# First rows turned at once, tile 0's norms moved ahead of other work, the last V sets halved between two engines

## What is computed

```python
n = rms_norm(h, attn_norm);  proj = n @ w_in          # c_q, c_kv, k_rope, dq, dk, dv
y_mla  = mla(...)      # 8 heads, q and k normed and rotated, causal softmax
y_diff = diff_attn(...)  # 4 heads, a = softmax1 - lam * softmax2; y normed (subln)
h = h + concat(y_mla, y_diff) @ w_out
x = rms_norm(h, ffn_norm)                             # "h1" in the kernel
q = x @ w_query;  s = q . sub_keys                    # PEER: 8 heads, 2 x 128 keys
best, flat = top16 of the 16 x 16 pair sums;  experts = e1 * 128 + e2
g = softmax(best);  act = gelu(x . u[experts])
h = h + sum over 8*16 slots of g * act * v[experts]   # gathers of 128 rows x 4 KB
```

## Time and profile before

| | us |
|---|---|
| three runs | 1487.81, 1499.03, 1493.09 (median 1493.09) |
| profiled execution, its own time | 1485.78 |
| its span, first to last instruction | 1484.1 |
| PE, DVE, POOL, ACT busy | 1214.9, 1040.1, 579.8, 425.3 |
| start to first gather issued | 206.3 |
| first gather to the last V set added (L2166 ends) | 206.3 to 894.2 |
| next block, to the end of the span | 894.2 to 1484.1 |

### The profile page before, as it was taken

How to read it: one execution, slowest core, us unless ns; L and a number is a source line. 1 busy time by engine, 2 the same in 40 slices (tenths; PEclk the granted TensorE clock), 3 DMA queues, 4 the chain that set the end, 5 groups by cost and what they waited for, 6 DMA issues and landing times.

```text
span 1484.1 us, 17603 instructions
## 1 busy us (share of the span) xinstructions
PE 1214.9 (82%) x6525; PEld 878.9 (59%) x6525; DVE 1040.1 (70%) x1910; ACT 425.3 (29%) x741; POOL 579.8 (39%) x644
## 2 busy tenths in 40 slices
PE   6987996687786555566765578999999999999997
PEld 3545674344443222222222237989889999899997
DVE  5786468888688775866656646677778888665556
ACT  1147213021112110211111114333345555343332
POOL 4140026777777777777777742001010000000000
PEclk9999898789998888777777789999999999999999
DMA  9917149999999999999999987778759565345662
GB/s 324 359 50 255 55 169 349 396 409 405 409 409 407 407 404 400 409 409 410 409 409 410 409 338 246 255 270 282 266 190 324 185 208 176 114 142 187 204 200 74
DMA packets 179996, 435.45 MB, mean 293 GB/s; under 512 B 13913, under 2 KB 84642, under 8 KB 179926
## 3 DMA queue, kind: packets, MB, share of 16 engines
q0 software_dynamic: 84384, 306.26, 52.5%
q1 hardware_dynamic: 94502, 126.18, 25.4%
q10 hardware_dynamic: 1040, 2.10, 0.4%
HBM read 433.44 MB, written 2.14 MB: 294 GB/s over the span
## 4 chain that ended last, share of the span: by engine, by line
PE 42%; POOL 30%; issue 11%; DVE 9%; DMA 5%; ACT 3%; SPq 0%; DVEq 0%; POOLq 0%
POOL arena L797 22%; PE quad L1507 13%; POOL ring L797 7%; PE quad_a L1613 7%; PE quad_a L1521 6%; DMA ring<-in_ffn_w_gu_dram 3%; PE quad_a L1307 2%; PE quad L1289 2%; PE quad_a L1206 2%; PE quad_a L1461 2%; PE quad_a L1678 2%; PE quad_a L1693 1%; DMA arena<-in_w_ada_dram 1%; PE quad_a L1535 1%; DMA arena<-in_peer_v_dram,arena 1%
## 5 line engine op out<-in xcount | busy, mean ns | idle before, releaser
L1461 PE MATMUL quad_a<-arena 128*128 128x512 f32 x384 | 205.9, 701 | 119.2 <-DMA arena<-in_peer_v_dram,arena 119.2
L1461 PEld LDWEIGHTS quad_a<-arena 128*128 128x128 f32 x384 | 85.8, 228 | 238.6 <-issue 238.3
L797 POOL DMA_INDIRECT arena<-in_peer_v_dram,arena x193 | 186.6, 967 | 60.7 <-issue 57.8
L1507 PE MATMUL quad<-u_hi,w_hi 128*128 128x256 f32 x704 | 198.8, 282 | 3.3 <-DVE u_lo L2044 3.3
L1507 PE MATMUL quad<-u_lo,w_hi 128*128 128x256 f32 x704 | 198.7, 282 | 0.0
L1507 PE MATMUL quad<-u_hi,w_lo 128*128 128x256 f32 x704 | 198.6, 282 | 0.0
L1983 DVE TENSOR_TENSOR w_lo<-ring,w_hi 128x2048 fp32r<-128x2048 f32 x66 | 150.8, 2290 | 62.3 <-ACT w_hi L995 62.0
L797 POOL DMA_INDIRECT arena<-in_peer_u_dram,arena x168 | 170.3, 1014 | 58.1 <-issue 50.6
L989 ACT ACTIVATE arena<-ident,arena 128x128 f32<-128x128 f32 x192 | 59.6, 389 | 341.9 <-DVE arena L2149 341.9
L2159 DVE SCALAR_TENSOR_TENSOR hx<-arena,hx 128x1024 f32<-128x1024 f32 x46 | 59.1, 1285 | 136.3 <-DMA arena<-in_peer_v_dram,arena 136.0
L2142 DVE CUSTOM_DVE_ANT_0 arena<-arena,quad_a 128x1024 f32<-128x1024 f32 x123 | 147.2, 1219 | 8.1 <-DMA arena<-in_peer_u_dram,arena 4.8
(11 more groups left out here) (387 smaller groups left out, 2394.0 us busy)
## 6 DMA issues: line engine op xcount, KB each, us to landing
ring<-in_ffn_w_gu_dram SPq DMA_DIRECT2D x44, 1024.0 KB, 8.9
arena<-in_w_ada_dram POOLq DMA_DIRECT2D x60, 512.0 KB, 6.6
ring<-in_ffn_w_down_dram SPq DMA_DIRECT2D x22, 1024.0 KB, 5.0
ring<-in_w_mix_in_dram SPq DMA_DIRECT2D x20, 1024.0 KB, 7.1
arena<-in_peer_w_query_dram SPq DMA_DIRECT2D x4, 2048.0 KB, 9.7
ring<-in_w_ada_dram POOLq DMA_DIRECT2D x12, 512.0 KB, 11.8
arena<-in_w_in_dram SPq DMA_DIRECT2D x3, 2048.0 KB, 35.8
arena<-in_w_out_dram SPq DMA_DIRECT2D x2, 2048.0 KB, 11.5
```

The lines of the kernel that those rows point to most:

```text
L797: gp.indirect_dma_start(out=rows_of(n), out_offset=None, in_=t["peer_" + kind][0], in_offset=bass.IndirectOffsetOnAxis(ap=expert[tt][:, sl ...
L1461: last = te.matmul(sum_side[tt][:, cols], diag[:, i % DIAGS], rows_of(n)[:, cols], start=(slot == pe_slots[0]), stop=(slot == pe_slots[-1] ...
L1507: last = te.matmul(psum[c][:, w * SEQ:(w + 1) * SEQ], weight[a][:, k, (c % 2) * P:(c % 2 + 1) * P], (u_hi, u_lo)[b][:, k], start=(k == 0 a ...
```

## The change

1. **Start.** x's tile 0 is squared, normed and turned before the others; the gains' turn moves from lane d to lane a and comes after it; six of the 16 small gain loads (`gain_src[3:]`) move from SP's queue to ACT's, behind the 2 MB load. PE does chunk "c" of tile 0 before it turns x's tiles 1 and 2.
2. **y of tile 0.** Its squares come before weighted(5), its root on ACT before turned_out(4), its norm and turn still in step 6; PE waits for it, turns it and does values(4) ahead of scores(7). turn_probs(5) moves behind write_out(0, 0), turn_probs(6) behind values(5), values(6) and values(7) behind the turn of hn.
3. **h1 of tile 0 by halves.** Squares of half 0 after the first half of the output, put into the root as its bias; hn is written in two instructions, each with a count of its own.
4. **Fewer DVE steps in `pick`**, and for two heads `row_of` is one reduction instead of four adds.
5. **The last 16 slots of tile 1** go in turn to PE and DVE (8 and 8) instead of 12 and 4.

```diff
@@ -127,6 +127,7 @@
 small = sb("small", 256)[:]
+h1_half, h1_bias = small[:, 200:201], small[:, 201:202]
@@ -251,10 +252,12 @@
+    if (tt, slot) >= (QT - 1, SLOTS - 2 * GB):
+        return slot % 2 == 0
     return slot % 4 != 3
-pe_slots = [slot for slot in range(SLOTS) if on_pe(0, slot)]
-diag_at = {(tt, slot): i for i, (tt, slot) in enumerate((tt, slot) for tt in range(QT) for slot in pe_slots)}
+pe_slots = [[slot for slot in range(SLOTS) if on_pe(tt, slot)] for tt in range(QT)]
+diag_at = {(tt, slot): i for i, (tt, slot) in enumerate((tt, slot) for tt in range(QT) for slot in pe_slots[tt])}
 diag_list = list(diag_at)
@@ -431,16 +434,16 @@
-d_jobs = ["gains"] + [("nT", tt, b) for tt in range(3) for b in range(2)] + [("fill", 0), ("fill", 1)] + [("cT", tt) for tt in range(3)]
+d_jobs = [("nT", tt, b) for tt in range(3) for b in range(2)] + [("fill", 0), ("fill", 1)] + [("cT", tt) for tt in range(3)]
 for i in range(len(STEPS)):
+    if i == 7:
+        d_jobs += [("yT", 0), ("o", 4)]
     d_jobs += [("s", i, m) for m in range(4)]
-    if i >= 3:
+    if 3 <= i < 7:
         d_jobs.append(("o", i - 3))
-    if i == 7:
-        d_jobs.append(("yT", 0))
-d_jobs += [("wo", n, 0) for n in range(2)] + [("o", i) for i in (5, 6, 7)]
-d_jobs += [("hnT", 0, b) for b in range(2)] + [("yT", 1)] + [("wo", n, 1) for n in range(2)]
-a_jobs = [("c", tt) for tt in range(3)] + [("rope", tt) for tt in range(3)] + [("dk", tt) for tt in range(3)]
+d_jobs += [("wo", n, 0) for n in range(2)] + [("o", 5)] + [("hnT", 0, b) for b in range(2)]
+d_jobs += [("o", 6), ("o", 7), ("yT", 1)] + [("wo", n, 1) for n in range(2)]
+a_jobs = ["gains"] + [("c", tt) for tt in range(3)] + [("rope", tt) for tt in range(3)] + [("dk", tt) for tt in range(3)]
 a_jobs += [("dq", tt) for tt in range(QT)]
@@ -566,6 +569,11 @@
+def gain_of(name):
+
+    src = t[name].rearrange("a b -> (a b)") if len(t[name].shape) == 2 else t[name].rearrange("a b c -> (a b c)")
+    return src.rearrange("(k p) -> k p", p=P)
+
 block = ctx.enter_context(nc.Block())
@@ -573,9 +581,8 @@
     sp.wait_ge(consts.sem, 1)
-    for name, n in gain_src:
-        src = t[name].rearrange("a b -> (a b)") if len(t[name].shape) == 2 else t[name].rearrange("a b c -> (a b c)")
-        sp.dma_start(gain_rows[GAIN[name]:GAIN[name] + n], src.rearrange("(k p) -> k p", p=P)).then_inc(ld_gain, 16)
+    for name, n in gain_src[:3]:
+        sp.dma_start(gain_rows[GAIN[name]:GAIN[name] + n], gain_of(name)).then_inc(ld_gain, 16)
     sp.dma_start(gain_rows[conv_row:conv_row + 12], t["conv_w_2"][0].rearrange("a (k p) -> (a k) p", p=P)).then_inc(ld_gain, 16)
@@ -831,6 +838,9 @@
     ac.dma_start(w_slot[0], t["w_in"][0].rearrange("(k p) n -> p k n", p=P)[:, :, C_C:C_C + 512]).then_inc(ld_c, 16)
+    sc_e.wait_ge(consts.sem, 1)
+    for name, n in gain_src[3:]:
+        ac.dma_start(gain_rows[GAIN[name]:GAIN[name] + n], gain_of(name)).then_inc(ld_gain, 16)
     sc_e.wait_ge(consts.sem, 9)
@@ -930,12 +940,14 @@
             evac_heads(*LATER[i])
+        if i == 6:
+            root(("subln", 0))
         if i >= 2:
             turned_out(i - 2)
-        if i == 6:
-            root(("subln", 0))
     turned_out(6)
-    root(("h1", 0))
+    k, cols, _ = norm_at["h1", 0]
+    sc_e.wait_ge(sums.sem, k + 1)
+    roots.mark(ac.activation(rstd[:, cols], stats[:, cols], ACT.Sqrt, bias=h1_bias, scale=1.0 / D))
     turned_out(7)
@@ -1174,10 +1186,7 @@
     pe.wait_ge(consts.sem, 9)
-    pe.wait_ge(ld_gain, 16 * (len(gain_src) + 7))
-    bank = d_bank("gains")
-    d_full.mark(flip(bank, 0, gain_rows, P, P))
-    for tt in range(3):
+    def turn_x(tt):
         pe.wait_ge(xn_ready.sem, tt + 1)
@@ -1185,6 +1194,10 @@
             d_full.mark(last)
+
+    turn_x(0)
+    pe.wait_ge(ld_gain, 16 * (len(gain_src) + 7))
+    a_full.mark(flip(a_bank("gains"), 0, gain_rows, P, P))
@@ -1208,7 +1221,10 @@
     pe.wait_ge(ld_c, 16)
-    chunk("c", w_slot[0], 512, range(3))
+    chunk("c", w_slot[0], 512, (0,))
+    for tt in (1, 2):
+        turn_x(tt)
+    chunk("c", w_slot[0], 512, (1, 2))
     pe.wait_ge(ld_hot, 32)
@@ -1380,31 +1396,31 @@
             pe.wait_ge(a_free.sem, a_at["dqT", QT - 1] + 1)
+        if i == 7:
+            pe.wait_ge(y_ready.sem, 1)
+            turn_y(0)
+            values(4)
         scores(i)
...
             turn_diff_heads()
-        if i >= 3:
+        if 3 <= i < 7:
             values(i - 3)
...
             turn_heads(*LATER[i])
-        if i == 7:
-            pe.wait_ge(y_ready.sem, 1)
-            turn_y(0)
-        if i >= 2:
+        if 2 <= i < 7:
             turn_probs(i - 2)
...
     write_out(0, 0)
-    turn_probs(6)
+    turn_probs(5)
     write_out(1, 0)
     values(5)
-    turn_probs(7)
-    values(6)
-    values(7)
+    for i in (6, 7):
+        turn_probs(i)
@@ -1415,9 +1431,11 @@
-    pe.wait_ge(hn_ready.sem, 1)
     for b in range(2):
+        pe.wait_ge(hn_ready.sem, b + 1)
         turn_hn(0, b, d_bank(("hnT", 0, b)), d_full)
+    values(6)
+    values(7)
     pe.wait_ge(d_free.sem, d_at["hnT", 0, 1] + 1)
@@ -1458,8 +1476,8 @@
                 cols = slice(512 * half, 512 * half + 512)
-                last = te.matmul(sum_side[tt][:, cols], diag[:, i % DIAGS], rows_of(n)[:, cols], start=(slot == pe_slots[0]),
-                                 stop=(slot == pe_slots[-1]), skip_group_check=True)
+                last = te.matmul(sum_side[tt][:, cols], diag[:, i % DIAGS], rows_of(n)[:, cols], start=(slot == pe_slots[tt][0]),
+                                 stop=(slot == pe_slots[tt][-1]), skip_group_check=True)
             last.then_inc(rows_used[buffer_of[n]], 1)
@@ -1470,7 +1488,7 @@
         if group == NORM1_AT:
-            pe.wait_ge(hn_ready.sem, 2)
+            pe.wait_ge(hn_ready.sem, 3)
             for b in range(2):
@@ -1730,17 +1748,41 @@
-    for tt in range(3):
+    def x_rows(tt):
         r = ROWS[tt]
-        src = hx[:, tt] if tt < QT else hm
+        return r, (hx[:, tt] if tt < QT else hm)[0:r]
+
+    def x_squared(tt):
+        r, src = x_rows(tt)
         ve.wait_ge(ld_x[tt], 16)
-        sums.step(ve, v.tensor_tensor_reduce(out=tmp[0:r], in0=src[0:r], in1=src[0:r], scale=1.0, scalar=0.0,
+        sums.step(ve, v.tensor_tensor_reduce(out=tmp[0:r], in0=src, in1=src, scale=1.0, scalar=0.0,
                                              op0=ALU.mult, op1=ALU.add, accum_out=stats[0:r, tt:tt + 1]))
-    for tt in range(3):
+
+    def x_normed(tt):
+        r, src = x_rows(tt)
+        xn_ready.mark(v.tensor_scalar(xn[0:r, tt], src, invert(("x", tt), r), None, ALU.mult))
+
+    def x_turned(tt):
         r = ROWS[tt]
-        src = hx[:, tt] if tt < QT else hm
-        inv = invert(("x", tt), r)
-        xn_ready.mark(v.tensor_scalar(xn[0:r, tt], src[0:r], inv, None, ALU.mult))
+        for b in range(2):
+            bank = take(("nT", tt, b))
+            g = GAIN["attn_norm"] + 4 * b
+            d_free.mark(v.tensor_tensor(nT[:, 4 * b:4 * b + 4, COL0[tt]:COL0[tt] + r],
+                                        bank[:, 0:4 * r].rearrange("p (k n) -> p k n", k=4),
+                                        spread(gains[:, g:g + 4], P, 4, r), ALU.mult))
+
+    x_squared(0)
+    x_normed(0)
+    for tt in (1, 2):
+        x_squared(tt)
+    bank = full_bank(ve, "gains", a_at, lane_a, a_full)
+    gains_ready.step(ve, v.tensor_copy(gains, bank[:, 0:P]))
+    a_free.mark(v.tensor_copy(small[:, 0:1], bank[:, 0:1]))
+    x_turned(0)
+    for tt in (1, 2):
+        x_normed(tt)
+    for tt in (1, 2):
+        x_turned(tt)
@@ -1760,18 +1802,6 @@
             ada_next[0], ada_at[s, m] = n + 1, n
-
-    bank = take("gains")
-    gains_ready.step(ve, v.tensor_copy(gains, bank[:, 0:P]))
-    d_free.mark(v.tensor_copy(small[:, 0:1], bank[:, 0:1]))
-    for tt in range(3):
-        r = ROWS[tt]
-        for b in range(2):
-            bank = take(("nT", tt, b))
-            g = GAIN["attn_norm"] + 4 * b
-            d_free.mark(v.tensor_tensor(nT[:, 4 * b:4 * b + 4, COL0[tt]:COL0[tt] + r],
-                                        bank[:, 0:4 * r].rearrange("p (k n) -> p k n", k=4),
-                                        spread(gains[:, g:g + 4], P, 4, r), ALU.mult))
@@ -1872,12 +1902,15 @@
-    def y_normed(tt):
+    def y_squared(tt):
         ve.wait_ge(d_free.sem, d_free.sent)
...
         sums.step(ve, v.tensor_reduce(stats[:, cols], y_sq[tt], AX, ALU.add))
+
+    def y_normed(tt):
+        yd = y[:, tt].rearrange("p (h c) -> p h c", h=DH)
         y_ready.mark(v.tensor_tensor(yd, yd, spread(invert(("subln", tt)), P, DH, DV), ALU.mult))
@@ -1941,30 +1974,49 @@
     for i in range(len(STEPS)):
+        if i == 7:
+            values_out(4)
         masked_scores(i)
+        if i == 6:
+            values_out(3)
+            y_squared(0)
         if i:
...
             step(v.tensor_scalar(lam[:, 0:1], lam[:, 2:3], LAMBDA_INIT, lam[:, 3:4], ALU.add, ALU.subtract))
-        if i >= 3:
+        if 3 <= i < 6:
             values_out(i - 3)
...
             y_normed(0)
```

(43 more changed lines are left out.)

## The result

Twenty runs of each kernel: before 1493.2 us (1487.81 to 1499.03), after 1498.07 us (1490.79 to 1500.98). The ratio is 1.003, 95% interval 1.0017 to 1.0043: the change costs 2.5 to 6.4 us. It was forecast to save 2. The profiled execution after took 1498.68 us (span 1496.2), near its median; the one before, 1485.78, was 7.4 under its own. So the two traces lie further apart than the kernels: 12.1 us, of which 6.2 arise before the first product of the second block's FFN and 5.9 behind it. There nothing is changed; PE is busy 573.0 us after and 567.1 before, at a granted clock of 0.97 or 0.98 in some windows of 100 us that have 1.00 before. Over the traces of this study this unchanged stretch takes 584.5 to 595.0 us, so the 5.9 us aren't charged to the change.

What follows compares the result with a forecast made beforehand. Bound by a chain of waits between engines, then PE, then full DMA gathers of fixed length, then PE's tail: -1.2 + 1.7 + 0 - 2.6 = -2.1 us, predicted median 1491.0, range 1484 to 1499.

Steps and rivals of the forecast that it cites:

- rival 2: Last V sets: PE's clock stays low or falls back in the gaps; +5.6 us, 1498.7; chance 0.13.
- Start: Up to DVE's last w_ada sum: gains complete at 13.3, big loads issued sooner; -1.2 us, range -1.8 to +0.5.
- Steps 6 and 7: Attention: earlier y starts write_out(0, 0) at 154.4, -2.5 us; output ends at 169.8, -1.8.
- T: End of the attention output, forecast at 169.8 us instead of 171.61.
- Output to query: Output's end to tile 0's first query: PE waits 2.4 us for hn, clock loses 1.2; attention to query +1.7.
- Rival 3: Late gains at 15.2 and the hn wait costing its full 1.8 us of clock; +1.1 us, 1494.2; chance 0.18.
- upper bound of attention: Attention to first query: the worst end of the range -2.1 to +2.6 us around +1.7.
- Pick: Before the gathers: fewer DVE steps only land the first eight sooner, the ninth waits for ACT; 0 us, up to -1.
- sign named for the gathers: Gathers: the ninth one's wait would be longer and the first eight would come sooner.
- Last sets: Tail: alternating sets between PE and DVE starts the final add at 890.4 instead of 892.99; -2.6 us, bounds -2.6 and +5.1.
- three signs of being wrong: PE not waiting for hn, a set taking PE 3.5 in the tail, or a POOL wait after 253.

Runs made afterwards that it cites:

- warm_y: nudge plus 28 overwritten identity turns on PE where it waits for y; ratio to the kernel before 0.9940. A: time from attention step 0 to step 5's values.
- busy: The kernel after with 20 overwritten identity turns on PE where it waits for the second norm's first half; ratio to the kernel before 0.9996.
- after_again: The kernel after, unchanged, run again on a faster chip; ratio to the kernel before 1.0034.
- p_attn: The kernel before with the two attention parts alone (y of tile 0, h1 of tile 0 by halves); ratio to the kernel before 1.0049.
- root_first: The kernel after with ACT's root of the second norm moved ahead of the copies of step 6; ratio to the kernel before 1.0004.
- nudge: The kernel after with the second norm's root ahead of step 6's copies on ACT and a POOL wait before its second memset; ratio to the kernel before 0.9984.
- attn_rf: The kernel before with the two attention parts alone and ACT's second-norm root ahead of step 6's copies; ratio to the kernel before 0.9981.
- attn_tail: The kernel before with the attention parts, ACT's root ahead, the halved last sets and POOL's wait, without start and pick; ratio to the kernel before 0.9996.
- flip6: The kernel after with turn_probs(6) back between the output halves; ratio to the kernel before 0.9999.
- preload: The kernel after with a spare-column root ahead of step 6's copies, so ACT's table load stands there; ratio to the kernel before 1.0021.

## Why the prediction was wrong

The median after, 1498.07, lies within the range of 1484 to 1499. That is no merit of the sum: the range reached so far up for rival 2, the cold tail, which didn't happen, and for the spread of the median. The sum had the sign wrong. Its own steps, with what the runs showed:

- **Start, -1.2.** Measured +0.1 at step 0, ratio 1.0004 alone. The gains were complete at 14.4, between the 13.3 taken and the bound of 15.2. PE's two waits (3.61 and 1.93 us) were followed by a chunk of 8.91 for 7.0. The DMA gain that the sum rested on didn't arrive: w_ada's last sum started at 69.80, not at 68.
- **Steps 6 and 7, write_out(0, 0) -2.5, T -1.8.** The first is right (154.58, -2.3). The second is not: -0.6, and in the other profile of the same kernel, counted from step 0, -0.2. The half starts sooner but at the lower level, 8.35 us instead of 7.27. The step forgot that an earlier start takes place earlier in the cold stretch. With the level kept up, as in warm_y, A is 3.5 us shorter.
- **Output to query, the failed step.** The mechanism is right in each link: copies, load, root over at T + 5.1 (foreseen 4.9), hn's first half at T + 6.1 (5.8), a wait of 2.78 for the 2.4 foreseen. The term that was mis-sized is "0 to 1.8, I take 1.2", for the wait that "costs the clock too". It measured 3.6 ahead of the query (busy) and 0.9 to 2.4 within it. The size came from the earlier trace rows, 12 matmuls after a wait of 2.89. There the level was back after some 3.4 us, so the 1.8 was all that this wait cost:

```profile
238.00:240.00 2.00, 1.64 (x3) 0.82 (x4) 2.00 (x3) 1.72 (x6) 0.64 (x1) 0.82 1.03 418
240.00:242.00 2.00, 2.00 (x4) 0.82 (x3) 2.00 (x5) 0.00 (x0) 1.39 (x3) 0.50 0.96 373
242.00:244.00 2.00, 2.00 (x6) 0.77 (x5) 2.00 (x5) 0.00 (x0) 1.69 (x2) 0.82 0.98 360
```

The step took this one stretch for the most that a wait can cost. Behind the same wait of 2.78 us for hn the lower level held for some 13 us (after) and 10 us (after_again, p_attn). A row with a long stretch stood in the earlier trace rows: after 4.35 us without work all of values(4) took 3.42, and the output half, 6 us later, was still slow at its beginning (7.27).
- **Rival 3** had this mechanism ("a long low clock") and the right sign for attention, but the same cap of 1.8. The upper bound of attention, +2.6, which it uses, is 0.3 more than its own terms give (0.5 + 1.8 = 2.3).
- **Pick, 0.** Not tried by itself. With the new order and the root ahead, the first gather comes 25.4 us behind the query with the new pick (root_first, nudge and others) and 25.8 without (attn_rf, attn_tail), and the ninth waits for ACT 3.8 us or more in either case, so what it wins is covered, as foreseen. The sign named for the gathers didn't come: in the kernel after the first one is issued 7.7 us later and the ninth waits 3.88 us, less than before.
- **Last sets, -2.6.** Final add -2.5, as foreseen, and rival 2 (a cold tail) is out: PE kept 1.95 a set. What no step had is the work behind it: 1.3 us by POOL's and DVE's meeting, and 3.4 to 3.8 us for the 16 products (after, flip6, preload, after_again) that had taken 2.05 in the profile before. This second part isn't shown to come from the change: with the old tail they took 2.6 to 3.8 in the four traces from slower chips. The saving was counted at the final add and not at the first instruction of the next stage. And it hangs on the arrival of the sets: the other traces with the old tail would have had 0, 1.9, 2.3 and 3.3 us to win.

Together, for the traces, at the second block's first FFN product: +6.2 where -2.1 was foreseen. Of the 8.3 between them 3.0 are the clock behind the wait for hn (3.6 ahead of the query and 0.6 that is left of the slow query at the gelu, against 1.2), 2.3 the tail, 1.3 the start, 1.2 T, and 0.5 the other links from the output to the query. So the failed step is the largest, but by itself it would have turned -2.1 only into +0.9. The medians differ by 4.9, with an interval of 2.5 to 6.4. None of the three signs of being wrong came as they were named (PE waited for hn, a set took 1.95, POOL's last wait is the old one, 6.5 later): they tested the links, not the length of the low stretch.

## What to carry to other kernels

When PE is given a new wait, price it by the stretch that follows, at half speed until the upper level is back, and not by the wait. One row isn't enough for that length: 3.4 to 13 us followed waits of about the same size here, so take the longest that the trace shows as the bound. If the wait can't be moved, put harmless matmuls in it that end before it does (28 turns, 3.2 us of idle time, brought 0.3 to 0.6% together with the two repairs, which alone had brought 0.1 to 0.2%). Before an instruction that needs a table load is put behind others on ACT, look whether the load was hidden until now: exchanging two statements was worth 6.8 us on the way to the query. Measure a saving at the next stage's first product, not at the instruction that was made earlier.

## What the runs showed of the hardware

- A wait of 1.36 us on PE was followed by some 10 us at the lower granted level (preload), one of 2.78 by 13 (after, 178 to 191) and 10 (after_again and p_attn), one of 2.89 by 3.4 (the kernel before, at 238), one of 0.94 (the kernel before, ahead of the query) by none: 7.41 us for the 64 matmuls against 7.31 without a wait. The length of the low stretch does not follow from that of the wait.
- The same unchanged second block took 584.5 to 595.0 us from its first FFN product on, in 20 traces.
- A DVE instruction on 128x128 took 1.54 or 1.55 us instead of 0.28 or 0.29 when it started at most 0.02 us behind a DMA issue of POOL that a memset followed, in seven traces.
- A product of two 128x128 float32 arrays stands in the trace as two matmuls, 0.23 us in all; a turn of the same size as one, 0.115, both at the upper level.
- Chips ran the same gathers at 406 to 409 or at 360 to 383 GB/s, 5% of the whole time.
